# A one-core decoder layer: where its first x tile, norm weights, small table and warm-up tile are made and placed

## The reference

```python
def rms_norm(x, gain, eps=NORM_EPS):
    y = xf * lax.rsqrt(jnp.mean(xf * xf, axis=-1, keepdims=True) + eps)
    return (y * gain.astype(jnp.float32)).astype(x.dtype)

def swiglu_ffn(x, gain, w_gate, w_up, w_down):
    h = rms_norm(x, gain)
    return (jax.nn.silu(h @ w_gate) * (h @ w_up)) @ w_down

x = x + 0.5 * swiglu_ffn(x, ffn1_norm[l], ffn1_w_gate[l], ffn1_w_up[l], ffn1_w_down[l])
```

## Time and profile before

| | us |
|---|---|
| median of 3 runs | 994.4 (994.15 to 994.59) |
| the profiled execution | 994.35 |
| its span, first to last instruction | 992.5 |
| TensorE busy | 987.5 |
| VectorE, ScalarE, GpSimd busy | 685.7, 444.7, 509.7 |

### The profile page before, as it was taken

The page is one execution under the profiler, slowest core; times in us unless marked ns, Lnnn a source line. Parts: engine busy times, 40 slices in busy tenths (PEclk is TensorE's granted clock), DMA queues, the critical chain, the costliest instruction groups (busy, mean ns, idle before and its releaser), DMA issues.

```text
span 992.5 us, 16521 instructions
## 1 busy us (share of the span) xinstructions
PE 987.5 (99%) x6833; PEld 872.2 (88%) x6833; DVE 685.7 (69%) x1092; ACT 444.7 (45%) x655; POOL 509.7 (51%) x297
## 2 busy tenths in 40 slices
PE   9999999999999999999999999999999999999998
PEld 7888999999999988788877888888999999999997
DVE  6894976676666497863547764789986676666745
ACT  8642444344443472534456764634343334433341
POOL 0355775676656433543252301645975666756741
PEclk9999999999999999999999999999999999999999
DMA  8432322332123312321221001322132333123312
GB/s 312 154 130 79 128 86 86 128 128 97 74 86 127 114 57 86 127 86 43 85 87 44 3 2 44 127 85 86 50 122 85 128 128 118 53 86 127 128 43 85
DMA packets 15914, 95.33 MB, mean 96 GB/s; under 512 B 2016, under 2 KB 2400, under 8 KB 5600
## 3 DMA queue, kind: packets, MB, share of 16 engines
q1 hardware_dynamic: 15696, 94.23, 26.4%
q10 hardware_dynamic: 144, 0.05, 0.0%
HBM read 92.17 MB, written 2.10 MB: 95 GB/s over the span
## 4 chain that ended last, share of the span: by engine, by line
PE 96%; DVE 3%; POOL 1%; issue 0%; ACT 0%; DVEq 0%; POOLq 0%
PE bank L2016 50%; PE bank L2142 35%; PE bank L2456 1%; PE bank L2542 1%; PE bank L2460 1%; PE bank L2482 1%; PE bank L2570 1%; PE bank L2559 1%; PE bank L2504 1%; PE bank L2194 1%; POOL wlo L517 0%; PE bank L2526 0%; DVE t_ffn_sum L1339 0%; PE bank L2606 0%; PE bank L2516 0%; PE bank L2628 0%
## 5 line engine op out<-in xcount | busy, mean ns | idle before, releaser
L2142 PE MATMUL bank<-t_ffn_hi,whi 128*128 128x256 f32 x952 | 269.4, 283 | 0.0
L2142 PE MATMUL bank<-t_ffn_hi,wlo 128*128 128x256 f32 x952 | 269.4, 283 | 0.0
L2142 PE MATMUL bank<-t_ffn_lo,whi 128*128 128x256 f32 x952 | 269.4, 283 | 0.0
L534 POOL TENSOR_TENSOR wlo<-sums,whi 128x512 fp32r<-128x512 f32 x136 | 184.7, 1380 | 131.8 <-ACT whi L739 131.7
L517 POOL TENSOR_TENSOR wlo<-raw,whi 128x1024 fp32r<-128x1024 f32 (+1 forms) x36 | 124.6, 3478 | 166.2 <-ACT whi L614 151.3
L534 POOL TENSOR_TENSOR wlo<-raw,whi 128x512 fp32r<-128x512 f32 x102 | 168.4, 1665 | 41.0 <-ACT whi L739 41.0
L2142 PEld LDWEIGHTS bank<-t_ffn_hi,whi 128*128 128x128 f32 x952 | 182.7, 192 | 0.7
L2142 PEld LDWEIGHTS bank<-t_ffn_lo,whi 128*128 128x128 f32 x952 | 182.7, 192 | 0.7
L2142 PEld LDWEIGHTS bank<-t_ffn_hi,wlo 128*128 128x128 f32 x952 | 182.7, 192 | 0.0
L2016 PE MATMUL bank<-ahi,whi 128*128 128x512 f32 x396 | 156.5, 395 | 0.4 <-POOL wlo L517 0.4
L2016 PE MATMUL bank<-ahi,wlo 128*128 128x512 f32 x396 | 154.4, 390 | 0.0
(11 more groups left out here) (339 smaller groups left out, 1405.1 us busy)
## 6 DMA issues: line engine op xcount, KB each, us to landing
raw<-fast_in SPq DMA_DIRECT2D x34, 1024.0 KB, 4.9
raw<-stream SPq DMA_DIRECT2D x26, 1024.0 KB, 4.9
raw_down<-fast_in SPq DMA_DIRECT2D x19, 1024.0 KB, 7.0
raw<-stream SPq DMA_DIRECT2D x7, 512.0 KB, 7.9
out<-x SPq DMA_DIRECT2D x7, 256.0 KB, 2.0
x<-x_in SPq DMA_DIRECT2D x3, 512.0 KB, 8.7
memx<-mem_in SPq DMA_DIRECT2D x2, 512.0 KB, 11.1
raw_gate<-stream SPq DMA_DIRECT2D x1, 1024.0 KB, 5.0
```

The costliest lines, as they stand in the source:

```text
L534: nc.gpsimd.tensor_tensor(in_ring(wlo, ring_at, n), whole[:, PIECE * at:PIECE * (at + 1)], in_ring(whi, ring_at, n).bitcast(F32), ALU.subt ...
L2142: ins = E.matmul(psum[bank][:, HALF * h:HALF * (h + 1)], a, b[:, k, :], start=start and k == 0 and m == 0, stop=k == K2 - 1 and m == 2, sk ...
```

## The change

- The array `x_in` gets 8 columns ahead of x: the weights of the first norm. One tile, `xg`, takes both, and `x` becomes a view of it that starts 32 bytes in. x's first piece carries the 8 columns along; `col` with a negative number reads them. `small` is 8 columns shorter, and its numbers shift.
- `small` is issued by SP behind the five pieces and ahead of memory, in place of by ScalarE ahead of everything. ScalarE waits for it ahead of `gain_qk`, VectorE behind the last piece's low parts.
- The high part of x's k tile 0 is written by VectorE, with a TENSOR_SCALAR ahead of its first low part of weights, and no longer by ScalarE.
- TensorE takes k tiles 0, 1 and 2 term by term, with a wait for each term's operand; k tiles 3 to 7 go on bank by bank.
- `warm` is 128 columns wide in place of 512. A warm-up matmul reads it four times over, for 512 columns as before, and there are 10 in place of 11.

```diff
--- before.py
+++ after.py
@@ -62,8 +62,8 @@
 C_BLK = C_SEL + 2
 C_PICK = C_BLK + 8
 C_N = C_PICK + 12
-S_G1, S_GM, S_G2, S_GMEM = 0, KD, 2 * KD, 3 * KD
-S_CONV = 4 * KD
+S_G1, S_GM, S_G2, S_GMEM = -KD, 0, KD, 2 * KD
+S_CONV = 3 * KD
 S_OG = S_CONV + 12 * 4
 S_MQ, S_MK, S_CQ, S_CK = S_OG + 1, S_OG + 2, S_OG + 3, S_OG + 4
 S_ALOG = S_OG + 5
@@ -99,7 +99,8 @@
             return ctx.enter_context(nc.semaphore(name))
 
 
-        x, _, _ = place("x", [P, KD, T])
+        xg, _, _ = place("xg", [P, KD + KD * T])
+        x = xg[:, KD:KD + KD * T].rearrange("p (k t) -> p k t", k=KD)
         ahi, a_hi0, _ = place("ahi", [P, KD, T], F32R)
         alo, a_lo0, _ = place("alo", [P, KD, T], F32R)
         raw, _, _ = place("raw", [P, RAW, 2048])
@@ -185,7 +186,7 @@
         memhi, _, nxt = place("memhi", [P, KD, M], F32R, at=nxt)
         memlo, _, nxt = place("memlo", [P, KD, M], F32R, at=nxt)
         memsq, _, _ = place("memsq", [P, KD, M], at=cq_at)
-        warm, _, _ = place("warm", [P, T], F32R, at=mid)
+        warm, _, _ = place("warm", [P, P], F32R, at=mid)
         msum, _, _ = place("msum", [P, M], at=at_at + 3 * M * 4)
         p6_at = nxt2
         mksq, _, nxt2 = place("mksq", [P, 2, M], at=nxt2)
@@ -252,7 +253,7 @@
             return psum[bank][:, M:T].rearrange("p (j q t) -> p j q t", j=2, q=2)
 
         def col(c):
-            return small[:, c:c + 1]
+            return small[:, c:c + 1] if c >= 0 else xg[:, KD + c:KD + c + 1]
 
         def places(pos, n):
 
@@ -445,7 +446,9 @@
                 k0, k1 = PIECES[i], PIECES[i + 1]
                 u, c0, c1, n = first_piece(i)
                 part(u, c0, c1, raw_in[u] if i in ENDS else w0_in[n])
-                sp.dma_start(x[:, k0:k1, :], x_in[:, k0:k1, :]).then_inc(x_sem[i], 16)
+                x0, x1 = KD + k0 * T if k0 else 0, KD + k1 * T
+                sp.dma_start(xg[:, x0:x1], x_in[:, x0:x1]).then_inc(x_sem[i], 16)
+            sp.dma_start(small[:], small_in).then_inc(small_sem, 16)
             for i in range(2):
                 sp.dma_start(memx[:, 4 * i:4 * i + 4, :], mem_in[:, 4 * i:4 * i + 4, :]).then_inc(mem_sems[i], 16)
             sp.wait_ge(w_lo, 1)
@@ -600,8 +603,6 @@
         @block.scalar
         def _(act):
             A = nc.scalar
-            A.dma_start(small[:], small_in).then_inc(small_sem, 16)
-
             def weight_hi(u):
 
                 act.wait_ge(raw_in[u % RAW], u // RAW * 16 + 16)
@@ -649,16 +650,17 @@
                     part_hi(u, c0, c1, raw_in[u], 16, w_hi)
                 else:
                     part_hi(u, c0, c1, w0_in[n], 16, piece_hi)
-                if i == 0:
-                    act.wait_ge(small_sem, 16)
                 act.wait_ge(x_sem[i], 16)
-                for d in range(PIECES[i], PIECES[i + 1]):
+                for d in range(max(PIECES[i], 1), PIECES[i + 1]):
+                    if d == 1:
+                        act.wait_ge(a_hi, 1)
                     x_high(0, S_G1, d)
                 if i > 0:
                     for d in range(PIECES[i - 1], PIECES[i]):
                         x_square(0, d)
             for d in range(PIECES[NP - 1], KD):
                 x_square(0, d)
+            act.wait_ge(small_sem, 16)
             A.activation(gain_qk[:, 0:1], col(S_MQ), ACT.Copy, scale=col(S_MK)).then_inc(gain_ready, 1)
             A.activation(gain_qk[:, 1:2], col(S_CQ), ACT.Copy, scale=col(S_CK)).then_inc(gain_ready, 1)
             for i in range(2):
@@ -1230,16 +1232,17 @@
                                            in1=memhi[:, k, :].bitcast(F32), op0=ALU.mult,
                                            op1=ALU.subtract).then_inc(mem_lo, 1)
 
+            dve.wait_ge(x_sem[0], 16)
+            V.tensor_scalar(x_hi[0][:, 0, :], x[:, 0, :], col(S_G1), None, ALU.mult).then_inc(a_hi, 1)
             for i in range(NP):
                 u, c0, c1, n = first_piece(i)
                 if i in ENDS:
                     part_lo(u, c0, c1, w_hi, u + 1, w_lo)
                 else:
                     part_lo(u, c0, c1, piece_hi, n + 1, piece_lo)
-                if i == 0:
-                    dve.wait_ge(small_sem, 16)
                 for d in range(PIECES[i], PIECES[i + 1]):
                     x_low(0, S_G1, d)
+            dve.wait_ge(small_sem, 16)
             dve.wait_ge(gain_ready, 2)
 
             def mem_sums():
@@ -2163,15 +2166,16 @@
 
             def first_pair():
 
-                pe.wait_ge(piece_hi, 1)
-                pe.wait_ge(a_hi, 1)
-                for (w, act_), (done, count) in zip(((whi, ahi), (wlo, ahi), (whi, alo)),
-                                                    ((a_hi, 1), (piece_lo, 1), (a_lo, 1))):
-                    pe.wait_ge(done, count)
-                    for bank in range(4):
-                        E.matmul(psum[bank][:], wslice(w, 0, 0, bank * P, P, PAIR), act_[:, 0, :],
-                                 start=w is whi and act_ is ahi, stop=False)
-                for k in range(1, KD):
+                for k in range(3):
+                    low = (piece_lo, k + 1) if k < 2 else (w_lo, 1)
+                    pe.wait_ge(*((piece_hi, k + 1) if k < 2 else (w_hi, 1)))
+                    for (w, act_), (done, count) in zip(((whi, ahi), (wlo, ahi), (whi, alo)),
+                                                        ((a_hi, k + 1), low, (a_lo, k + 1))):
+                        pe.wait_ge(done, count)
+                        for bank in range(4):
+                            E.matmul(psum[bank][:], wslice(w, 0, k, bank * P, P, PAIR), act_[:, k, :],
+                                     start=k == 0 and w is whi and act_ is ahi, stop=False)
+                for k in range(3, KD):
                     pe.wait_ge(a_hi, k + 1)
                     if k in PIECES:
                         i = PIECES.index(k)
@@ -2190,8 +2194,8 @@
                 n0, u0, d0 = 2 * FG * f, U_FFN[f], KD * FG * f
                 if f == 0:
                     pe.wait_ge(warm_ready, 1)
-                    for _ in range(11):
-                        E.matmul(psum[4][:], warm[:, 0:P], warm[:], start=True, stop=True)
+                    for _ in range(10):
+                        E.matmul(heads(4), warm[:], warm[:].unsqueeze(1).broadcast_to([P, H, P]), start=True, stop=True)
                     first_pair()
                     mem_keys_values()
                 else:
@@ -2943,7 +2947,7 @@
         return v.reshape(-1, P).T
 
     small = np.concatenate(
-        [per_partition(a[n][0]) for n in ("ffn1_norm", "mix_norm", "ffn2_norm", "mem_norm")]
+        [per_partition(a[n][0]) for n in ("mix_norm", "ffn2_norm", "mem_norm")]
         + [a["gdn_conv_w"][0].reshape(4, 12, P).transpose(2, 1, 0).reshape(P, 48), a["gdn_out_norm"][0][:, None]]
         + [np.concatenate([a[n][0]] * 2)[:, None] for n in ("moba_q_norm", "moba_k_norm", "mem_q_norm", "mem_k_norm")]
         + [np.broadcast_to(a[n], (P, H)) for n in ("gdn_a_log", "gdn_dt_bias")], axis=1)
@@ -2952,7 +2956,8 @@
     arrays = {
         "stream": np.stack(units),
         "fast_in": np.stack(fast),
-        "x_in": a["x"][0].T.reshape(KD, P, T).transpose(1, 0, 2),
+        "x_in": np.concatenate([per_partition(a["ffn1_norm"][0]),
+                                a["x"][0].T.reshape(KD, P, T).transpose(1, 0, 2).reshape(P, KD * T)], axis=1),
         "mem_in": a["mem"][0].T.reshape(KD, P, M).transpose(1, 0, 2),
         "ab_in": mv_ab[KD - 1],
         "small_in": small,
```

## The result

| us | before | changed |
|---|---|---|
| median of 6 runs each | 994.41 (994.15 to 994.59) | 998.75 (998.27 to 999.48) |
| the profiled execution, its span | 994.35, 992.5 | 998.47, 996.7 |
| first memory matmul starts | 28.52 | 28.13 |
| TensorE busy | 987.5 | 991.6 |

The ratio is 1.0045, with a 95% interval of 1.0034 to 1.0056: 4.3 us slower, and 3.75 us above the upper end of the range, 995.0. In the profiled execution the start gained about what was forecast of it; the time was lost where the diff has no line.

The account below looks back on a forecast made before the run. TensorE, busy 987.5 of 992.5 us, was taken as the bound. A gain of 0.2 at the start plus 0.08 from term order, 0.28, off 994.35 gave 994.07, as a median 994.1; range 993.5 to 995.0.

Parts of the forecast that it names:

- Warm-up tile: At the start: a 128-column tile takes 0.21 us, TensorE begins at 0.99 and ends ten warm-up matmuls at 5.42, not 6.17.
- First x tile: VectorE's high part takes 0.49 us, x lands 0.07 earlier, so the first real matmul starts at 5.96, 0.35 us earlier.
- two readings of the rise: TensorE's clock rise stays near 6.8 us, so the earlier start gains 0.17, or follows the warm-up, so it gains 0.35.
- Three tiles by terms: K tiles 0 to 2: low parts needed later, making the earlier start worth having and removing a 0.08 us hesitation.
- Small table: Issued by SP at 5.95, it moves mem's two issues back by about 0.45 us and costs nothing.
- I carry a shift at the start through to the end undiminished.: Later stages are fed by counts of TensorE's own work, so the start's gain reaches the kernel's end whole.
- Rival 3: Slower: tiles between x and small move 32 bytes; one cycle for each of 6833 loads, 2.8 us, 997; chance 0.03.
- Rival 2: Slower: 0.5 us idle after warm-up makes TensorE's clock rise late; +2.1 us, 996.5, or halfway 995.4; chance 0.08.
- Rival 1: At the start: VectorE takes 0.75 us or x lands late, so nothing is gained; 994.4; chance 0.18.

## Why the prediction was wrong

**The forecast, 994.1.** Wrong: 998.75 was measured. The terms that it sums up are not what failed. The start gained 0.39 us at memory's first matmul where 0.28 was summed up. With the placement undone the same start measured 994.1, and that is the forecast's number by luck in part, as the kernel before measured 994.31 beside it and the interval is 0.9990 to 1.0009. The gain is seen in the traces in which the first product's tiles keep their distance: memory's first matmul came at 27.98 to 28.38 in six with the new start and three tiles by terms (and at 30.34 in the one with the late rise), at 28.52 to 28.67 in three with the old one. It can't be told from nothing in the times. Over all traces the first real matmul came at 6.12 to 6.75 us with the new start and at 6.27 to 6.65 with the old one, so the scatter of x's landing is as large as the gain.

**Warm-up tile.** Right: 0.20 for the tile (0.21 forecast), first matmul at 0.99.

**First x tile.** The operation is right, 0.49. The landing is not: the forecast had it up to 0.18 earlier without the small table ahead, taken as 0.07. The weights' piece landed 0.56 earlier (ScalarE at 4.21, not 4.77), but x's at 5.5, 0.1 later than before, and at 6.1 in another execution. So the first real matmul was at 6.15, not 5.96. The clock made up for this by luck: in the changed kernel the load at 6.53 already takes 0.19 us, where the earlier trace rows has the slow one at 6.45 and the first fast one at 6.87. In six traces with the old warm-up from 1.31 us (before, and the experiments with its start) the last slow load begins anywhere from 4.0 to 7.2, so neither of the prediction's two readings of the rise can be confirmed from one pair of traces. The Trainium skill ("TensorE: Matmul & The Clock Gate", Part 1) has the watch on activity running freely; this scatter, at one and the same warm-up, agrees.

**Three tiles by terms.** Right: with one, k tile 2 waits for its low part, 0.6 us. More than said, as x's pieces now land later (ScalarE at 10.81 for k tile 2, has 10.22).

**Small table.** Right: ScalarE's first reader of it starts at 20.49, straight behind its squares (18.41 to 20.59), with no idle time. That this is 1.0 us later than the earlier trace rows comes from x's pieces, and memory's first matmul did not wait for it.

**"I carry a shift at the start through to the end undiminished."** No run speaks against it for the start's own shift. But the pace of all the rest was taken as given, and that is where the time went.

**Rival 3, placement, 0.03.** This is the step that failed. The prediction saw the 32 bytes and asked the right question, then priced it wrongly in three ways. First, it took it as a cost of a stationary tile by itself; the run with all tiles shifted shows no such cost. Second, it concluded from the earlier trace rows that moving tiles don't mind. Those rows have 264 columns, and their moving tiles, 1056 bytes apart, lie 0, 32, 64 and so on to 192 bytes off a multiple of 256, so only one place in seven is at distance 0 from the stationary tile. They are close to the width at which no distance costs (113.4 to 120.0 ns in the table, against 119.9 at 0), so they can say nothing of 512 columns. Nor do they show indifference: in the trace of before their steps scatter from 116 to 125 ns (but for one wait), while those of 256 columns are 120 almost to the last. (Durations move with the steps, 389.0 to 395.4 ns in the matmuls alone where the step goes from 226.7 to 233.3, so it was the sample that misled and not the measure.) Third, it bounded the cost at one cycle a load, 2.8 us, and gave it 0.03. It measured +6.1 ns for the 1050 matmuls of 512 columns with hidden values and some +6 for 240 more (memory, the second block's x), about +8, and about -1.8 for the 1656 of 256 columns whose t operands had not moved along, about -3; with -0.4 of the start that is +4.6, and the trace has +4.1. The rest are gaps of TensorE, most of them where the second block's seven-for-eight part begins: over the 210 matmuls from 690 to 721 us the starts leave 1.2 us over the pace in the trace before and 0.7 over the same ones in the trace after. A mechanism that touches nearly all of the instructions of the engine that is busy 99% of the time deserved a wider range than one that touches the first 12 us, however unlikely.

**Rival 2, the late rise.** A late rise was seen in one profiled execution of seven, 2.2 us later at memory's first matmul with x's own 0.6 in it (2.1 was the price for the clock alone), and is no part of the 4.3 us. That the gap brings it about is not shown. **Rival 1, start held.** x did land late, but the first real matmul of the changed kernel's trace was still 0.16 earlier than before; in the times, nothing gained can't be told from the small gain.

## What to carry to other kernels

Before growing a tile at the front of an arena, check what slides: keep the distance between weight and moving tiles modulo 256 bytes, or change it on purpose, by moving operand and by columns. Compare stretches of matmuls by their starts divided by the count, and take a small change of the mean duration seriously: it is the same number of ns on a smaller step. An edit whose diff is in the first 12 us can cost 4 us in the other 980, and a layout that nobody chose may leave 8 us to be had.

## What the runs showed of the hardware that was not expected

The step of a stream of weight load and matmul (float32 data in the faster format) depends on the distance in bytes between the two SBUF tiles: 227 ns at 0 and 229 to 234 at any other multiple of 32 up to 224, with 512 columns; 120 at 0 and 113.4 to 120 elsewhere with 256 columns. Both moved together by 32, 64 or 128 bytes next to nothing changes (227.3 and 120.0 ns at most), and with 256 columns all 16 pairs of places at multiples of 256 up to 768 took 119.9 to 120.1. At 64 bytes the step with 256 columns has two values, 113.4 and 117.8; within one program what ran before picks one, the same way in both repetitions, and by what rule is not known. Why (which ports or banks are met at once) no run shows; nor is it known whether a layer could be made to enter its 256-column stretches in the faster state, which would be worth another (116.7 - 113.4) x 2856 = 9 us, an estimate from these steps.
